# First attention scores in free banks, an Exp table load moved, a transpose moved, and own places for eight weight pieces

## The reference

```python
h = modulate(x, shift, scale)                      # LN, times (1+scale), plus shift
p = h @ w_in                                       # one projection, columns split into groups A, B, C, D, and a gate
a = global attention over latent + context keys    # group A, 4 query heads, 2 key heads, q/k RMS-normed, rotary
b = windowed attention (+-128) + context keys      # group B, with a sink logit
f = DFT over positions and channels, then a map    # group C
r = two-way retention, group norm, * silu(gate)    # group D
x = post_norm(x, g1 * (concat(a, b, f, r) @ w_out))     # LN(ALPHA*x + y)
x = post_norm(x, g2 * swiglu(modulate(x, sh2, sc2)))    # gate/up and down projections
```

## Time and profile before

| | |
|---|---|
| median of three runs | 1804.92 us (1803.84 to 1806.47) |
| the profiled execution | 1806.75 us, its span 1804.9 us |
| mean granted clock of TensorE | 0.970 of full speed |
| PE busy | 1687.4 us, 93% of the span, 9038 matmuls |
| VectorE busy | 851.1 us, 47% |
| ScalarE busy | 465.9 us, 26% |
| GpSimd busy | 830.7 us, 46% |
| DMA | 164.94 MB, mean 91 GB/s |

### The profile page before, as it was taken

The page is one execution under the profiler, slowest core; times in us unless marked ns, Lnnn a source line. Parts: engine busy times, 40 slices in busy tenths (PEclk is TensorE's granted clock), DMA queues, the critical chain, the costliest instruction groups (busy, mean ns, idle before and its releaser), DMA issues.

```text
span 1804.9 us, 22786 instructions
## 1 busy us (share of the span) xinstructions
PE 1687.4 (93%) x9038; PEld 1375.5 (76%) x9038; DVE 851.1 (47%) x1248; ACT 465.9 (26%) x948; POOL 830.7 (46%) x820
## 2 busy tenths in 40 slices
PE   5999799999899999999999979897999799999997
PEld 3877666547799997799998768785737688778885
DVE  4353243556762513545454674734476521340048
ACT  5411454521710002200002163125531500210021
POOL 4443032412464443444445444622333597676772
PEclk8999899999999999999999999998999899999999
DMA  9211044302153411234552111210112363233321
GB/s 346 70 62 55 1 147 138 111 1 70 48 174 95 129 41 65 64 112 140 166 195 72 47 42 56 85 47 17 50 50 71 94 175 105 82 94 94 103 95 47
DMA packets 157295, 164.94 MB, mean 91 GB/s; under 512 B 6414, under 2 KB 111742, under 8 KB 156934
## 3 DMA queue, kind: packets, MB, share of 16 engines
q1 hardware_dynamic: 136566, 121.40, 21.7%
q10 hardware_dynamic: 20624, 42.09, 7.1%
HBM read 161.37 MB, written 2.10 MB: 91 GB/s over the span
## 4 chain that ended last, share of the span: by engine, by line
PE 82%; DVE 9%; ACT 6%; issue 2%; POOL 1%; DMA 0%; ACTq 0%; DVEq 0%; SPq 0%; POOLq 0%
PE ps L662 22%; PE ps L664 22%; PE ps L663 22%; PE ps L878 3%; PE ps L900 2%; ACT probs L1418 1%; PE ps L1030 1%; DVE act_lo L1729 1%; PE ps L1018 1%; PE ps L919 1%; DVE ps L1738 1%; DVE mod_acc_ffn L1924 1%; ACT hbuf L1321 1%; PE ps L759 1%; DVE st L1746 1%
## 5 line engine op out<-in xcount | busy, mean ns | idle before, releaser
L626 POOL TENSOR_SCALAR ring_hi<-stage 128x512 fp32r<-128x512 f32 x368 | 263.0, 715 | 709.8 <-PE ps L664 679.7
L629 POOL TENSOR_TENSOR ring_lo<-stage,ring_hi 128x512 fp32r<-128x512 f32 x368 | 511.0, 1389 | 30.7
L662 PE MATMUL ps<-act_hi,ring_hi 128*128 128x384 f32 (+2 forms) x1168 | 405.9, 348 | 5.3 <-POOL ring_lo L629 5.3
L663 PE MATMUL ps<-act_lo,ring_hi 128*128 128x384 f32 (+2 forms) x1168 | 403.3, 345 | 0.0
L664 PE MATMUL ps<-act_hi,ring_lo 128*128 128x384 f32 (+2 forms) x1168 | 403.3, 345 | 0.0
L662 PE MATMUL ps<-ring_hi,act_hi 128*128 128x512 f32 (+1 forms) x748 | 298.8, 399 | 22.7 <-DVE act_lo L1729 9.7
L664 PE MATMUL ps<-ring_hi,act_lo 128*128 128x512 f32 (+1 forms) x748 | 291.3, 389 | 0.0
L663 PE MATMUL ps<-ring_lo,act_hi 128*128 128x512 f32 (+1 forms) x748 | 291.1, 389 | 0.0
L662 PEld LDWEIGHTS ps<-act_hi,ring_hi 128*128 128x128 f32 x1168 | 222.8, 191 | 18.9 <-POOL ring_lo L629 6.0
L663 PEld LDWEIGHTS ps<-act_lo,ring_hi 128*128 128x128 f32 x1168 | 222.7, 191 | 13.1
L664 PEld LDWEIGHTS ps<-act_hi,ring_lo 128*128 128x128 f32 x1168 | 222.5, 190 | 13.1
(11 more groups left out here) (222 smaller groups left out, 1909.1 us busy)
## 6 DMA issues: line engine op xcount, KB each, us to landing
stage<-in_w_gate_up_dram SPq DMA_DIRECT2D x88, 512.0 KB, 5.0
mod_stage<-in_w_mod_dram ACTq DMA_DIRECT2D x56, 512.0 KB, 4.1
stage<-in_w_in_dram SPq DMA_DIRECT2D x18, 1024.0 KB, 5.0
stage<-in_w_down_dram SPq DMA_DIRECT2D x16, 1024.0 KB, 4.9
stage<-in_w_mod_dram SPq DMA_DIRECT2D x12, 1024.0 KB, 5.1
start_mod<-in_w_mod_dram SPq DMA_DIRECT2D x8, 1024.0 KB, 12.3
stage<-in_w_down_dram SPq DMA_DIRECT2D x8, 768.0 KB, 4.3
stage<-in_w_out_dram SPq DMA_DIRECT2D x16, 256.0 KB, 4.7
```

Source lines behind the costliest of these rows:

```text
L626: nc.gpsimd.tensor_scalar(ring_hi[:, g % RING, :], stage[:, par, j * 512:(j + 1) * 512], 1.0, 0.0, ALU.mult, ALU.add).then_inc(w_hi, 1)
L629: nc.gpsimd.tensor_tensor(ring_lo[:, g % RING, :], stage[:, par, j * 512:(j + 1) * 512], ring_hi[:, g % RING, :].bitcast(F32), ALU.subtrac ...
L662: nc.tensor.matmul(o, a_hi, b_hi, start=first, stop=False)
L663: nc.tensor.matmul(o, a_hi, b_lo, start=False, stop=False)
```

## The change

It has four parts.

1. *Scores of pair 0.* They go to bank 4 + a in layer 0, and to banks 4 to 7 in layer 1, in place of banks 0 to 3. The attention begins without a wait for the Silus; in layer 0 it waits for the transposed tiles of blocks 0 and 1 only. The waits for all Silus and all transposed tiles stand at step 1, and step 1 no longer waits for pair 0's Exp.
2. *Exp table.* A one-column Exp stands behind the last Silu, so that the table is loaded there.
3. *wout of layer 1.* Tile 0's transposes stand behind the fourth k-piece of the last tile, no longer behind its eighth.
4. *Own places.* The first eight pieces of layer 1's win go to `own_hi` and `own_lo`, which lie where `hid` was, and not through the ring. GpSimd splits them when VectorE has split the last hidden piece. All later slots move up by eight: block 1's pieces take the ring slots that block 0's had.

The core of the diff (the loop headers and the signatures that follow from it are left out):

```diff
--- before.py
+++ after.py
+def segment(key):
+    return [-4] * 2 + [4] * 7 if key == (1, "win") else SEGMENTS[key[1]]
@@ plan()
-        unit0[key], slot0[key] = len(units), slots
-        for i, n in enumerate(SEGMENTS[key[1]]):
-            slots += n
+        unit0[key], slot0[key] = len(units), slots - (8 if key == (1, "win") else 0)
+        for i, n in enumerate(segment(key)):
+            slots += max(n, 0)
             mods += n == 0
+            own += max(-n, 0)
...
+            units.append((key, n, own if n < 0 else slots, mods, sent[len(units) % 2]))
@@ build(), places
+        own_at = [PR + 12288 + 4096 * e for e in range(6)] + [PR, PR + 4096]
+        own_hi = [place(f"own_hi{e}", [P, 512], R32, offset=own_at[e]) for e in range(8)]
+        own_lo = [place(f"own_lo{e}", [P, 512], R32, offset=own_at[e] + 2048) for e in range(8)]
@@ unit_release_wait()
-            if n:
+            if n < 0:
+                e.wait_ge(own_ready, slots)
+            elif n:
                 e.wait_ge(w_ready, slots)
@@ new
+        def score_banks(l, i, a):
+            if i:
+                return ps[:, 2 * a:2 * a + 2, :].rearrange("p b n -> p (b n)")
+            if l < DEPTH - 1:
+                return ps[:, 4 + a, :]
+            return ps[:, 4 + 2 * a:6 + 2 * a, :].rearrange("p b n -> p (b n)")
@@ GpSimd, for each unit
+                for i, n in enumerate(segment((l, seg))):
                     unit_wait(pool, u0)
+                    if n < 0:
+                        need(pool, "hid_split", l - 1, 4 * HALF)
+                        for j in range(-n):
+                            e, part = 4 * i + j, stage[:, u0 % 2, j * 512:(j + 1) * 512]
+                            nc.gpsimd.tensor_scalar(own_hi[e][:, :], part, 1.0, 0.0, ALU.mult, ALU.add).then_inc(own_hi_ready, 1)
+                            pool.wait_ge(own_hi_ready, e + 1)
+                            nc.gpsimd.tensor_tensor(own_lo[e][:, :], part, own_hi[e][:, :].bitcast(F32),
+                                                    ALU.subtract).then_inc(own_ready, 1)
+                        g0 -= n
@@ TensorE, project(l), l > 0, block 0
-                            pe.wait_ge(w_ready, g + j + 1)
+                            pe.wait_ge(own_ready, j + 1)
...
-                                         ring_hi[:, (g + j) % RING, w], ring_lo[:, (g + j) % RING, w], j == 0, j == KC - 1)
-                            if n == NT - 1:
-                                mm.then_inc(ring_used, 1)
-                            elif j == KC - 1:
-                                mm.then_inc(sem("win_acc"), 1)
+                            mm = product(ps[:, t, w], act_hi[:, j, s], act_lo[:, j, s], own_hi[j][:, w], own_lo[j][:, w],
+                                         j == 0, j == KC - 1)
+                            if j == KC - 1:
+                                mm.then_inc(sem("own_used") if n == NT - 1 else sem("win_acc"), 1)
@@ TensorE, attention(l)
-                    if 0 < s <= total:
+                    if 1 < s <= total:
                         need(pe, "probs_ready", l, 2 * s)
                     if s == 1:
                         need(pe, "gate_silu", l, 2 * len(token_parts(l)))
+                        need(pe, "qk_read", l, sum(len(block_tiles(l, b)) for b in range(4)))
@@ TensorE, last_pass()
-                    if n >= 3 and key != (DEPTH - 1, 2):
+                        if nt == 4 and n == 3 and j == 3 and key != (DEPTH - 1, 2):
+                            transposes(key, 0)
+                    if nt > 4 and n >= 3 and key != (DEPTH - 1, 2):
                         transposes(key, n - 3)
@@ TensorE, layer loop, ahead of attention(l)
-                need(pe, "gate_silu", l, 2)
-                need(pe, "qk_read", l, sum(len(block_tiles(l, b)) for b in range(4)))
+                need(pe, "qk_read", l, sum(len(block_tiles(l, b)) for b in range(4 if l else 2)))
@@ ScalarE, project(l)
-                        if n == len(tiles) - 1:
+                        if n == len(tiles) - 1 and b == 0 and l > 0:
+                            act.wait_ge(sem("own_used"), 1)
+                        elif n == len(tiles) - 1:
                             act.wait_ge(ring_used, win_last_slot(l, b) + 1)
...
                         a.activation(gate_ret[:, c, c0:c0 + width], ps[:, 2 * c + r, 0:width], ACT.Silu).then_inc(sem("gate_silu"), 1)
+                a.activation(silu_warm[:, :], eps[:, :], ACT.Exp)
```

14 lines of the change are left out of this document (6 added, 8 removed).

## The result

The changed kernel takes 1787.6 us in the median of four runs (1784.2 to 1790.5), beside 1805.5 us for the kernel before on the same chip: a ratio of 0.9901, 95% interval 0.9878 to 0.9924. Six more runs later gave 1786.1 us and 0.991 (0.9892 to 0.9927). So the gain is 16 to 18 us; 13.7 were forecast. The profiled execution took 1785.15 us.

What follows compares the result with a forecast made beforehand. PE, with 82% of the last-ending chain, nearly all unchanged matmuls, was taken as the bound. Terms 4.8 + 2.4 + 2.7 + 3.8 = 13.7 off the median 1804.92 gave 1791.2 us; eight-in-ten range 1787.5 to 1797.

Steps and rivals of the forecast that it cites:

- all upper ends: All parts at their best: 5.2 + 3.3 + 2.8 + 5.6 = 16.9 us, giving 1788.0, not expected all at once.
- 4, block 1: Layer 1's projection, block 1: VectorE's latent tiles at 4.6 us, PE's waits down to 0.8; gain 4.8 us.
- 4, norm: Norm ending layer 0: longer idle before tile 4's transposes may keep tile 1's matmuls at low clock; cost 1.0 us.
- rival (f): Attentions: ScalarE empties itself between a Silu and the table load, at most 0.74 us per layer; 1792.7 us; chance 0.03.
- one term: Layer 0's attention: pair 2's scores at the full 2.93 us in place of 2.06, taking 0.9 from 3.3.
- two of the signs: Block 1 of layer 1's projection: VectorE's latent tiles under 5 us, and under 1 us of waits for the rotated tile.
- Rival (b): Norm ending layer 0: own splits beside VectorE's first tiles delay the norm by about 3 us; 1794 us; chance 0.05.
- the cover of 5.70: Norm ending layer 0: ScalarE's 5.70 us wait for tile 0's transposes, expected to absorb VectorE's delay of 2.7.
- (a): Block 1: splits coming singly slow VectorE like a burst, costing 3 to 5 of 4.8 us; 1794 to 1797; chance 0.2.
- (c): Attentions: PE stays at low clock, some 4.2 us more per step; with five steps 1812 us, slower; chance 0.02.
- (d): Attentions give half: two or three more low-clock pieces per layer, 1.4 us each; about 1795 us; chance 0.1.
- (e): Attentions: first scores still wait for a late semaphore, gains shrink to 0.5 and 1.3; 1796.6 us; chance 0.03.

Runs made afterwards that it cites:

- both mends: The changed kernel with the edits of tile1_early and copies_first together (also written both_mended): 1781.8 us, ratio 0.9876.
- light_splits: The changed kernel with GpSimd subtracting only 16 of 512 columns for the low halves of block 2's eight pieces in layer 1's win: 1783.2 us, ratio 0.9888.
- copies_first: The changed kernel with ScalarE copying out block 1's accumulators of tiles 0 to 4 before block 0's last transposed tile: 1787.1 us, ratio 0.9893.
- scores_only: The kernel before with pair 0's scores in their own banks alone: 1794.9 us, ratio 0.9943.
- after_again: The changed kernel measured and profiled once more, nothing edited: 1786.1 us, ratio 0.991.
- table_only: The kernel before with the one-column Exp behind the gate Silus alone: 1800.8 us, ratio 0.9985.
- before_d16: The kernel before with sixteen more matmuls at the start of block 2 of layer 0's projection: 1806.8 us, ratio 1.0013.
- own_only: The kernel before with own places for the first eight slots of layer 1's projection alone: 1802.5 us, ratio 0.9984.
- after: The changed kernel with all four parts, in its first measurement and profile: 1787.6 us, ratio 0.9901.
- tile1_early: The changed kernel with the norm's transposes of tiles 3 and 4 behind the eighth slots of tiles 0 and 1: 1789.7 us, ratio 0.9912.
- after_d16: The changed kernel with sixteen more matmuls at the start of block 2 of layer 0's projection: 1793.6 us, ratio 0.9939.

## Why the prediction was right

The time of 1787.6 us lies 3.6 below the forecast of 1791.2. It is inside the range of 1787.5 to 1797 by 0.1 us, below the forecast's own range of 1788.5 to 1794, and below the 1788.0 of all upper ends together. The working does not reach that far, so that the time still fell inside the range is luck. What the working can be held against are the stages. Of all fourteen profiles, with and without a part, the means are (both mends left out where they act; light_splits left out of block 1 and of what lies behind it, copies_first of the latter):

| part | forecast | profiled pair | means of the stages |
|---|---|---|---|
| 1, attention 1 | 4.8 | 5.06 | 27.98 - 23.03 = 4.95 |
| 2, attention 0 | 2.4 | 3.61 | 34.79 - 30.89 = 3.90 |
| 3, wout | 2.7 | 2.58 | 36.21 - 33.99 = 2.22 |
| 4, block 1 | 4.8 | 4.04 | 41.13 - 37.24 = 3.89 |
| 4, norm | -1.0 | -0.96 | 37.45 - 38.39 = -0.94 |
| 4, behind block 1 | 0 | -1.63 | 73.20 - 73.97 = -0.77 |
| sum | 13.7 | 12.7 | 13.25 |

That the sums come this near to 13.7 is in part luck too: part 2 gave 1.2 to 1.5 more than its term, and part 4 gave 1.6 to 2.4 less.

**Part 1** held step by step: from the last transposed key's copy to the reciprocal 5.1 was worked out and 5.20 measured, to pair 1's maximum 5.4 and 5.29, and pair 2's scores at half clock, 2.93. The table load behind the Silus has no drain in front of it in any trace: 1207.89 behind 1207.88. The Trainium skill (ScalarE: Activation LUTs, What ACT_TABLE_LOAD costs) gives a drain of 1.38 us per switch; these traces do not agree, and rival (f) is out. (The 3.6 that the prediction gives for that case took the 1.38 off in full; with the maximum at 1225.2 coming later than the table, 1.1 would have gone, so 3.7.)

**Part 2 is mis-sized in one term.** The shift was right, 3.57 for 3.3. The clock was taken with the wrong sign, -0.9: I argued that four microseconds without work would send pair 2's scores to 2.93. They took 1.66 after 3.82 idle, and 1.58 after 3.73 in scores_only. In the old order waits of 2.3 to 3.0 us stood in front of both pair 1's scores and pair 2's, and pair 1's ran at the low clock, pair 2's too or in part (2.93, 2.06). In the new order 1.37 us stand in front of the first and 3.7 to 3.8 in front of the second, and neither did. In layer 1 sixteen in one go and then a wait of 4.74 us were followed by 2.93. So the length of the last idle time alone did not decide. The stage's own gain, 3.4 to 5.3 us by kernel, spreads with the low clock behind these scores.

**Part 3** held: 2.58 and 2.71 in the two closest pairs, though after_again (34.49) and others show less, and the means give 2.22.

**Part 4 came out at 1.45 in the pair and 2.2 in the means, for 3.8.** Block 1's mechanism held: latent tiles of 4.8 to 5.8 us, waits of 1.36 in place of 4.0. It was under the 4.8 because the tiles took 4.8 to 5.8 where I had set 4.6 for each; two of the signs that I had set, tiles under 5 us and under 1 us of waits, were missed. And the low-clock stretch, put at 1.6 of block 1's loss, hid most of itself behind VectorE: in table_only and before_d16, where the clock stayed up in block 1 with the old slots, PE waited 4.9 us in three waits in place of 4.0 in two, and the block took 40.8 in place of 41.3. The wait in table_only:

```profile
PE ps L802 <- DVE post L1877: 4.9, 3, 2.8
```

The norm's cost, 1.0, was as worked out, in both of its readings: tile 4's transposes did not move, and tile 1 ran at the low clock; but with the old slots table_only and before_d16 take 38.01 and 38.30 for the norm too, beside 37.1 in the other four, so a part of this 1.0 may be the clock's own spread. Rival (b)'s mechanism was there, 2.5 us for the 2.7 worked out, and the cover of 5.70 took it. The Trainium skill (SBUF — State Buffer, SBUF: two separate sides) has VectorE with two SBUF inputs and GpSimd exclude each other; the rows of this norm agree, with numbers below. What the prediction left out is the start of block 2. Block 1's low-clock stretch was counted as won (the 1.6 of its 5.6), and what lies behind block 1 stood at nothing. With the stretch gone, the next wait of 1.90 us, which had been harmless, was followed by one of the same size in four of the six profiles with own places and that wait (own_only, after, after_again, tile1_early; not after_d16 and light_splits), and in two of the six without own places (table_only, before_d16), where block 1 had no low stretch of its own. In each of the twelve profiles that have the wait, no more than one of the two places is at the low clock. The stretch moved more than it went, by 0.8 us in the means and 1.63 in the pair; that removing the first brought on the second is argued from these counts, not shown. The step that failed is that nothing was asked of the wait behind the one removed; with that wait gone too, in copies_first and both_mended, the stage is 3.7 shorter.

**The rivals.** (a) did not come: the first three latent tiles took 5.8, 4.8 and 5.2 us (reciprocals at 1111.68, 1117.46, 1122.26 and 1127.42), after 8.0 and 6.8 before. light_splits shows that what slowness is left comes with GpSimd's second instruction. (c), (d) and (e) did not come either: attention 1 lost nothing more, and scores_only alone brought 3.8 and 5.3. The norm of layer 0 changed by 1.0, within the 2 us that were set as a sign of being wrong.

**What stays open** is the 3 to 5 us between the stages' 12.7 to 13.3 and the 16 to 18 of the medians. The stretch without any change took 830.9 to 839.6 us over fourteen profiles, with the same instructions. It took both long and short values with the old attention (839.58, 833.62) and with the new (839.01, 831.02, 830.94). So one profile can be off by 8.7 us, and a part of the surplus may be no more than that; the interval of the second measurement reaches down to 13.2. Part 4 is where it shows most: 7.0 us by the whole times with the new attention and 2.9 with the old, for 0.9 to 2.2 in the stages, and no run explains the difference between the two. Whether the changed kernel meets the short stretch more often than the kernel before, as the lower level of four in six runs suggests, the runs with the shifted work did not settle.

## What to carry to other kernels

Where pairs of work take turns in one set of buffers, a second set for the first of them alone moves up everything behind it for good: here 3.8 us of attention 1, with no other edit (scores_only). When a wait is taken away from a chain, look at the next one on the same engine, however harmless it was: its cost may grow by the low clock that had stood behind the first. Cut the traces by the same instructions and compare stages: attention 1 repeats to 0.4 us and block 1 to 0.5 among kernels with the same parts, where the unchanged stretch spreads by 8.7, so a part of 2 us is seen there and not in a median. Other stages spread more (the norm by 0.6 with own places and 1.2 without, wout by 1.4, attention 0 by 1.8), so one profile each is not enough for a part of under 1 us.

## What the runs showed of the hardware

- The granted clock fell to its lower level in places where PE was busy throughout (14.00 of 14 us at a clock of 0.76, above), and did not in the next execution (1.00). Such a place is 3.2 us long or short for the same instructions, and the whole unchanged stretch 8.7 us.
- VectorE's operations beside GpSimd's own splits, on the norm's first tiles: the scaled residuals, with two operands in SBUF, took 1852 ns in the mean where they had taken 1285, while those with an operand in PSUM did not change (700, and 686 to 687). Groups by line (busy us, mean ns of one), before and after:

```profile
L1801 DVE SCALAR_TENSOR_TENSOR resid<-resid,st,bc 128x1024 f32<-128x1024 f32 x2 | 2.6, 1285 | 0.1
...
L1742 DVE TENSOR_TENSOR resid<-resid,ps 128x512 f32<-128x512 f32 x3 | 2.1, 686 | 0.1
```
```profile
L1834 DVE SCALAR_TENSOR_TENSOR resid<-resid,st,bc 128x1024 f32<-128x1024 f32 x2 | 3.7, 1852 | 0.1
...
L1775 DVE TENSOR_TENSOR resid<-resid,ps 128x512 f32<-128x512 f32 x3 | 2.1, 687 | 0.1
```
